# Normed rows transposed inside the last quarter's products, roots on ScalarE alone, and a conv that begins with chunks 0 to 2

## Chip, cores and metric

One core of one Trainium2 chip runs the whole kernel in one launch. The metric is the device time of that core in microseconds (us), the median over the runs shown.

## What is computed

One step of a two-layer encoder over 544 frames of 1024 features: 512 of a new stream and 32 of a running one. Layer 0 is a norm, a combined projection, band attention beside a gated linear recurrence, an output projection and a residual, then a norm and a mixture of experts. Layer 1 has a gated short convolution in place of the mixers. Cut to what the change touches:

```python
def rmsnorm(x, gain):
    y = x * rsqrt(mean(x * x, axis=-1) + 1e-6)
    return y * gain

def short_conv(xn, w_in, conv_w, w_out, prev):      # layer 1
    bg, cg, h = split(xn @ w_in, 3)
    u = cg * h
    up = concat(prev, u)
    conv = up[0:T] * conv_w[0] + up[1:T+1] * conv_w[1] + up[2:T+2] * conv_w[2]
    return (bg * conv) @ w_out

def hier_moe(x, ...):                               # both layers
    grp = argmax(x @ w_group + b_group)             # top 1 of 4 groups
    topv, topi = top_k((x @ w_expert + b_expert)[grp], 2)   # top 2 of its 8 experts
    h = silu(x @ w1[e]) * (x @ w3[e]) * gates       # 32 experts, 1024 -> 256
    return sum over e of h @ w2[e]                  # 256 -> 1024
```

## The kernel before

**Tiling.** Frames lie in five chunks (NC), four of 128 and one of 32 rows (ROWS). H holds the residual stream, one chunk of rows per block. Features are on partitions in eight blocks (KT) for a product, so normed rows are transposed on TensorE first. Float32 products of the mixers are split: a tensor is copied to a rounded high part by ScalarE (..._hi) and the rest is taken by VectorE or GpSimd (..._lo), and three products hi*hi, lo*hi, hi*lo add up in one PSUM bank.

**Norms.** `norm(n, c)` is the norm n (0 and 2 before the mixers, 1 and 3 before the experts) of chunk c. ScalarE's `square` sums squares into ssq (L1036), VectorE makes mean plus epsilon (L1257), ScalarE takes the root (L1038), VectorE the reciprocal (L1259) and the product with row and gain (L1265) into XN (n even) or XF (n odd). For XF the features are re-ordered by the access pattern: it is written densely and H and the gain are read with a step of eight elements. `norm_transpose(n, c)` (L615) then makes eight transposes (L630) into two banks. For n odd ScalarE copies the low and VectorE the high half to XT (L1047, L1270). For n = 2 ScalarE makes xc_hi (L1059) and VectorE xc_lo (L1278).

**Order around the change.** Every engine's order is written out by hand, with semaphores between engines.

- `project_out` (L861): the output projection, in four quarters (OQ) of 256 columns times five chunks, 24 products each (L873), four banks in turn. `residual` on VectorE adds each result to H (L1523); in the last quarter it also calls norm 2n+1 of the chunk before. The splits of the quarters' weights stand in between (L1515).
- `mixture(l)` on TensorE (L883): all five transposes of norm 2l+1, with products of the identity that have no reader (`idle_products`, L613) ahead of chunks 2, 3 and 4; the router's product (L892) over XT; then `route` on VectorE, two small products, and from VectorE's indices GpSimd gathers rows of x from DRAM (L570) for two experts at a time. TensorE transposes these (L927) and runs the 32 experts in pairs (L933, L944).
- The sync queue stores XF's chunks to DRAM (x_rows, L420) as they are normed and loads expert weights into six slots of 24 KB a partition: three transfers of 1 MB an expert (L388 twice, L391). Experts 0 to 3 are sent for ahead of `mixture` (2 and 3 at the start of the last quarter), 4 and 5 behind the router's product, and expert e from 6 on when expert e-6's products are done.
- After the experts of layer 0 the queue reads both results of each row back (yab, L455). VectorE combines them into H (L1682, twice a chunk) with norm 2 of the chunk before in between. TensorE transposes all five chunks, and waits until all are split.
- The conv's products (L1013): a loop of four times two column blocks m, each with two halves of 272 frames; a half has three terms a (banks 3*half + a) of 24 products. ScalarE and VectorE turn each half into gst, g_hi and g_lo; `conv_hi` and `conv_lo` split the weights of coming blocks. `conv_out_hi(0)` and `conv_out_lo(0)` split the first quarter of the next output projection's weights ahead of the conv.

**Memory.** XT lies at 132 KB over XN and the start of XF. The five yab lie at 132 to 172 KB, over XN and XF, where xc_hi (152 KB) also is.

## Time and profile before

| | us |
|---|---|
| median of 3 runs | 1229.3 |
| the three runs | 1226.22, 1229.3, 1235.59 |
| profiled execution | 1231.18 |
| its span on the chip | 1229.4 |
| TensorE products busy | 1035.0 (84%) |
| VectorE busy | 434.6 (35%) |
| ScalarE busy | 282.9 (23%) |
| mean granted clock of TensorE | 0.912 of full |

The views come from one profiled execution. The page sums it up; the chain of waits follows the work that ended last back from the end, at each step to what released it; the timeline gives each instruction with its start, its length, and in brackets how long its engine had been idle and what ended that; windows give busy time, clock and DMA share of a stretch. An engine's busy share over the whole span says little, since the stages have different limits. A product of plain float32 comes as two records (28 for 14 idle products), a transpose as one. A line such as L1265 is a line of the kernel before.

### The profile page before, as it was taken

Reading aid. Unit: us, or ns where it says so; the run is one execution under the profiler, and the core shown is the slowest. Engines: PE = TensorE matmul, PEld = TensorE weight load, DVE = VectorE, ACT = ScalarE, POOL = GpSimd, SP = SyncE. Lnnn points to the kernel's source line nnn. Section 1 sums busy time; section 2 is a strip of 40 time slices with the busy share of each in tenths; the row PEclk is TensorE's granted clock in tenths of the full one; section 3 lists DMA queues with packets and bytes.
Section 4 is the critical chain, followed back from the end, with each engine's and each line's share of the span. In section 5 each row is a group of like instructions: output and inputs, shape, how many; then the busy total and the mean of one; then the engine's idle time right before and its main releaser. Section 6 shows DMA issues by size and latency. Waiting matters only on the chain.

```text
span 1229.4 us, 20254 instructions
## 1 busy us (share of the span) xinstructions
PE 1035.0 (84%) x8691; PEld 807.0 (66%) x8691; DVE 434.6 (35%) x935; ACT 282.9 (23%) x543; POOL 181.2 (15%) x146
## 2 busy tenths in 40 slices
PE   5998999777999899977887179999998899788771
PEld 4988999654599755444443179999997655344440
DVE  5324484357724611101100654655336111010104
ACT  4244322115722121111111322121212121111110
POOL 4234332002000012211111000000000122111110
PEclk9999999856999999989988579999999999988886
DMA  6322321401085769999997703324568699999966
GB/s 213 86 74 69 101 85 38 111 11 52 22 294 194 293 261 416 416 416 416 416 416 286 235 1 103 93 61 154 206 67 353 250 416 416 417 415 417 416 268 227
DMA packets 114855, 282.71 MB, mean 230 GB/s; under 512 B 22954, under 2 KB 70102, under 8 KB 98356
## 3 DMA queue, kind: packets, MB, share of 16 engines
q1 hardware_dynamic: 105044, 263.66, 57.9%
q0 software_dynamic: 9728, 17.85, 3.9%
q8 instruction: 63, 1.03, 0.4%
q14 instruction: 20, 0.16, 0.0%
HBM read 270.57 MB, written 27.02 MB: 242 GB/s over the span
## 4 chain that ended last, share of the span: by engine, by line
PE 57%; DMA 17%; DVE 10%; SPq 10%; ACT 2%; issue 2%; POOL 1%; DVEq 0%; POOLq 0%; ACTq 0%
DMA w<-in_w_dram 13%; PE banks L1013 12%; PE banks L933 11%; PE banks L655 8%; PE banks L873 8%; SPq L388 7%; PE banks L944 4%; PE banks L654 3%; SPq L391 3%; DMA wab<-in_w_in_ab_dram 2%; DVE H L1682 2%; DVE XF L1265 2%; PE banks L927 1%; POOL wab_lo L562 1%; PE banks L832 1%
## 5 line engine op out<-in xcount | busy, mean ns | idle before, releaser
L933 PE MATMUL banks<-w,xgT 128*64 128x256 f32 x2048 | 261.5, 416 | 68.5 <-DMA w<-in_w_dram 67.5
L933 PEld LDWEIGHTS banks<-w,xgT 128*64 128x64 f32 x2048 | 161.3, 150 | 176.9 <-DMA w<-in_w_dram 72.5
L1631 DVE TENSOR_TENSOR hh<-banks,sg 128x128 f32<-128x128 f32 x64 | 18.7, 292 | 410.6 <-ACT sg L1201 377.9
L574 POOL DMA_INDIRECT y_rows<-ys,yidx x64 | 63.8, 996 | 384.7 <-ACT ys L1209 379.8
L944 PE MATMUL banks<-w,hT 128*64 128x512 f32 x512 | 116.9, 598 | 0.0
L1013 PE MATMUL banks<-xc_hi,wc_hi 128*128 128x272 f32 x384 | 111.9, 291 | 1.4 <-DVE xc_lo L1278 1.4
L1013 PE MATMUL banks<-xc_hi,wc_lo 128*128 128x272 f32 x384 | 112.1, 292 | 0.0
L1013 PE MATMUL banks<-xc_lo,wc_hi 128*128 128x272 f32 x384 | 111.6, 291 | 0.0
L570 POOL DMA_INDIRECT xr<-x_rows,gidx x32 | 33.5, 1047 | 430.5 <-DVE yidx L1616 411.9
L655 PE MATMUL banks<-wab_hi,xc_hi 128*128 128x256 f32 (+1 forms) x320 | 91.3, 286 | 0.8 <-POOL wab_lo L562 0.8
L655 PE MATMUL banks<-wab_hi,xp_lo 128*128 128x256 f32 (+1 forms) x320 | 90.3, 283 | 0.0
L655 PE MATMUL banks<-wab_lo,xc_hi 128*128 128x256 f32 (+1 forms) x320 | 88.4, 280 | 0.0
L1201 ACT ACTIVATE sg<-banks 128x128 f32<-128x128 f32 x64 | 17.8, 278 | 296.6 <-PE banks L933 296.6
L562 POOL TENSOR_TENSOR wab_lo<-wab,wab_hi 128x2048 fp32r<-128x2048 f32 x14 | 67.3, 4813 | 122.4 <-ACT wab_hi L1052 122.4
L1013 PEld LDWEIGHTS banks<-xc_hi,wc_hi 128*128 128x128 f32 x384 | 73.5, 191 | 1.6 <-issue 1.5
L1013 PEld LDWEIGHTS banks<-xc_lo,wc_hi 128*128 128x128 f32 x384 | 73.5, 191 | 0.0
L1013 PEld LDWEIGHTS banks<-xc_hi,wc_lo 128*128 128x128 f32 x384 | 73.3, 191 | 0.0
L944 PEld LDWEIGHTS banks<-w,hT 128*64 128x64 f32 x512 | 34.0, 136 | 58.7 <-issue 54.8
L654 PE MATMUL banks<-xc_hi,wab_hi 128*128 128x272 f32 x192 | 57.1, 297 | 7.2 <-POOL wab_lo L562 7.2
L1209 ACT ACTIVATE ys<-banks 128x512 f32<-128x512 f32 x64 | 38.2, 597 | 97.9 <-PE banks L944 97.9
L655 PEld LDWEIGHTS banks<-wab_hi,xc_hi 128*128 128x128 f32 (+1 forms) x320 | 55.7, 174 | 1.7 <-POOL wab_lo L562 1.0
L654 PE MATMUL banks<-xc_hi,wab_lo 128*128 128x272 f32 x192 | 56.8, 296 | 0.0
(284 smaller groups left out, 1811.1 us busy)
## 6 DMA issues: line engine op xcount, KB each, us to landing
w<-in_w_dram SPq DMA_DIRECT2D x192, 1024.0 KB
wab<-in_w_in_ab_dram SPq DMA_DIRECT2D x13, 1024.0 KB, 5.2
wc<-in_w_in_c_dram SPq DMA_DIRECT2D x24, 512.0 KB
yab<-y_rows SPq DMA_DIRECT2D x16, 512.0 KB, 6.9
wo<-in_w_out_ab_dram SPq DMA_DIRECT2D x4, 1024.0 KB, 5.1
x_rows<-XF SPq DMA_DIRECT2D x8, 512.0 KB, 10.4
wo<-in_w_out_c_dram SPq DMA_DIRECT2D x4, 1024.0 KB, 5.7
H<-in_x_prompt_dram SPq DMA_DIRECT2D x4, 512.0 KB, 8.4
```

The lines of the kernel that those rows point to most:

```text
L388: sp.dma_start(w13[s][:, part, :, :], w[l, bass.ds(e, 1)].rearrange("e (p k) f -> p (e k) f", p=P)).then_inc(done, 16)
L391: sp.dma_start(w2s[s][:], w2[l, bass.ds(e, 1)].rearrange("e (a p) n -> p (e a) n", p=P)).then_inc(done, 16)
L562: pool.tensor_tensor(wab_lo[n % 3][:], wab[n % 3][:], wab_hi[n % 3][:].bitcast(F32), ALU.subtract).then_inc(w_lo, 1)
L570: pool.indirect_dma_start(xr[i][:, :], None, x_dram[l][:, :], bass.IndirectOffsetOnAxis(ap=index.bitcast(U32), axis=0), bounds_check=T - 1 ...
L574: pool.indirect_dma_start(y_dram[l][:, :], bass.IndirectOffsetOnAxis(ap=index.bitcast(U32), axis=0), ys[i][:, :], None, bounds_check=4 * T ...
L654: return pe.matmul(out, w[:, k, cols], x[:, k, t], **flags)
L655: return pe.matmul(out, x[:, k, t], w[:, k, :], **flags)
L873: last = pe.matmul(bank[i % 4][0:ROWS[c], 0:OW], z(a, k)[:, c * P:c * P + ROWS[c]], w(b, k, s), start=k == 0 and j == 0, stop=k == KT - 1 ...
L933: last = pe.matmul(bank[hb][64 * f:64 * f + 64, 0:2 * P].rearrange("p (w j) -> p w j", w=2), xgT[i][:, k, 64 * ab:64 * ab + 64], w13[s][:, ...
L944: last = pe.matmul(bank[6 + ab][64 * n:64 * n + 64, :], hT[ab][:, 64 * f:64 * f + 64], w2s[s][:, f, n * 512:(n + 1) * 512], start=f == 0, ...
L1013: last = pe.matmul(bank[3 * half + a][:, 0:HALF], w[s][:, k, a, :], x[:, k, half * HALF:(half + 1) * HALF], start=k == 0 and j == 0, stop= ...
L1209: act.activation(ys[e % 4][:], bank[6 + ab][:, :], ACT.Copy).then_inc(ys_ok, 1)
```

## The change

- **Roots.** ScalarE takes the root straight from ssq, with 1/D as scale and epsilon as bias. VectorE's mean and the semaphore ms_ok go.
- **The view of norms 1 and 3.** H and the gain are read densely and XF is written with a step of 128 elements; its layout is as before.
- **Transposes in the last quarter.** `project_out` calls `norm_transpose` of chunk c-2 behind the products of chunks 2, 3 and 4; chunks 3 and 4 follow in `mixture`. Six idle products stand ahead of chunk 4 and none elsewhere. ScalarE makes all XT copies but the high half of chunk 4.
- **XT** moves into the slot of expert 3, one tensor a layer. Expert 3 is sent for with 4 and 5, behind the router's product.
- **The conv's start.** Combines, norms and splits of chunks 0 to 2 come first, then those of 3 and 4. TensorE begins the first half's terms 0 and 1 when chunks 0 to 2 are split, transposes 3 and 4, runs term 2, and waits for all chunks ahead of the second half. Chunk 2's transposes go to banks 0 and 1. The loop over column blocks is written out. Three of the yab move behind 169 KB.
- **Weights of the output projection in layer 1.** The first quarter's split goes from ahead of the conv to its end.

```diff
--- before.py
+++ after.py
...
+CONV_BANKS = [6, 4, 0, 6, 4]
...
-        XT = at("XT", 132, [P, KT, T])
+        XT = [at(f"XT{l}", RING + 24 * SLOTS[l][3], [P, KT, T]) for l in range(2)]
...
-        yab = [at(f"yab{c}", 132 + 8 * c, [P, 2, D]) for c in range(NC)]
+        yab = [at(f"yab{c}", (132, 140, MISC, MISC + 8, MISC + 16)[c], [P, 2, D]) for c in range(NC)]
...
-                for j in (4, 5):
+                for j in (3, 4, 5):
                     first_load(l, j)
...
-            for j in (2, 3):
-                first_load(0, j)
+            first_load(0, 2)
             mixture(0)
...
-            for j in (2, 3):
-                first_load(1, j)
+            first_load(1, 2)
             mixture(1)
...
             def norm_transpose(n, c):
+                if n % 2 == 1 and c == 4:
+                    idle_products(1, 6)
                 pe.wait_ge(xn_ok, NC * n + c + 1)
-                if n % 2 == 1 and c >= 2:
-                    idle_products(1, 14 if c == 2 else 3)
                 if n == 0 and c == 0:
                     pe.wait_ge(pool_c, zeroed[0])
 
                 low = 6 if c % 2 == 0 else 4
-                if n % 2 == 0 and c > 1:
+                if n == 2:
+                    low = CONV_BANKS[c]
+                if n == 0 and c > 1:
                     pe.wait_ge(xt_d, NC * n + c - 1)
+                if n == 2 and c > 2:
+                    pe.wait_ge(xt_d, NC * n + c - 2)
                 for half in range(2):
                     if n % 2 == 1 and c > 1:
                         pe.wait_ge(xt_a if half == 0 else xt_d, NC * n + c - 1)
...
                     last.then_inc(op_mm, 1)
+                    if s == OQ - 1 and c >= 2:
+                        norm_transpose(2 * n + 1, c - 2)
...
             def mixture(l):
-                norm_transposes(2 * l + 1)
+                for c in (3, 4):
+                    norm_transpose(2 * l + 1, c)
                 pe.wait_ge(xt_a, NC * (2 * l + 2))
...
-                        last = pe.matmul(bank[0][p0:p0 + NR, 0:t.stop - t.start], wr[:, k, :], XT[:, k, t], start=k == 0, stop=k == KT - 1)
+                        last = pe.matmul(bank[0][p0:p0 + NR, 0:t.stop - t.start], wr[:, k, :], XT[l][:, k, t], start=k == 0, stop=k == KT - 1)
...
 
-            norm_transposes(2)
-            pe.wait_ge(xt_a, NC * 3)
-            pe.wait_ge(xt_d, NC * 3)
-            with pe.Fori(0, KT // 2) as i:
-                for s in range(2):
-                    pe.wait_ge(wc_lo_ok, i * 2 + (s + 1))
-                    for half in range(2):
-                        pe.wait_ge(cg_ok, i * 4 + (2 * s + half + 1))
-                        for a in range(3):
-                            for k in range(KT):
-                                for j, (w, x) in enumerate(((wc_hi, xc_hi), (wc_hi, xc_lo), (wc_lo, xc_hi))):
-                                    last = pe.matmul(bank[3 * half + a][:, 0:HALF], w[s][:, k, a, :],
-                                                     x[:, k, half * HALF:(half + 1) * HALF],
-                                                     start=k == 0 and j == 0, stop=k == KT - 1 and j == 2)
-                        last.then_inc(c_mm, 1)
+            def conv_terms(s, half, a):
+                for k in range(KT):
+                    for j, (w, x) in enumerate(((wc_hi, xc_hi), (wc_hi, xc_lo), (wc_lo, xc_hi))):
+                        last = pe.matmul(bank[3 * half + a][:, 0:HALF], w[s][:, k, a, :], x[:, k, half * HALF:(half + 1) * HALF],
+                                         start=k == 0 and j == 0, stop=k == KT - 1 and j == 2)
+                if a == 2:
+                    last.then_inc(c_mm, 1)
+
+            def frames_ready(c):
+                pe.wait_ge(xt_a, NC * 2 + c)
+                pe.wait_ge(xt_d, NC * 2 + c)
+            for c in range(3):
+                norm_transpose(2, c)
+            pe.wait_ge(wc_lo_ok, 1)
+            frames_ready(3)
+            for a in range(3):
+                if a == 2:
+                    norm_transpose(2, 3)
+                    norm_transpose(2, 4)
+                conv_terms(0, 0, a)
+            frames_ready(NC)
+            for a in range(3):
+                conv_terms(0, 1, a)
+            for m in range(1, KT):
+                pe.wait_ge(wc_lo_ok, m + 1)
+                for half in range(2):
+                    pe.wait_ge(cg_ok, 2 * m + half + 1)
+                    for a in range(3):
+                        conv_terms(m % 2, half, a)
...
                 act.activation(junk[:], H[:, c, :], ACT.Square, accum_out=ssq[:, c:c + 1]).then_inc(sq_done, 1)
-                act.wait_ge(ms_ok, NC * n + c + 1)
-                act.activation(rms[:, c:c + 1], rms[:, c:c + 1], ACT.Sqrt).then_inc(rt_ok, 1)
+                act.wait_ge(sq_done, NC * n + c + 1)
+                act.activation(rms[:, c:c + 1], ssq[:, c:c + 1], ACT.Sqrt, bias=epsc[:, 0:1], scale=1.0 / D).then_inc(rt_ok, 1)
...
-            def xt_low(n):
-                for c in range(NC):
-                    act.wait_ge(xt_mm, NXT * n + 2 * c + 1)
-                    act.activation(XT[:, 0:4, c * P:c * P + ROWS[c]],
-                                   bank[6 - 2 * (c % 2)][:, :].rearrange("p (k t) -> p k t", k=4)[:, :, 0:ROWS[c]], ACT.Copy).then_inc(xt_a, 1)
+            def xt_copy(n, c, half, done):
+                act.wait_ge(xt_mm, NXT * n + 2 * c + half + 1)
+                act.activation(XT[n // 2][:, 4 * half:4 * half + 4, c * P:c * P + ROWS[c]],
+                               bank[6 - 2 * (c % 2) + half][:, :].rearrange("p (k t) -> p k t", k=4)[:, :, 0:ROWS[c]], ACT.Copy).then_inc(done, 1)
...
-                    low = 6 - 2 * (c % 2)
+                    low = 6 - 2 * (c % 2) if n == 0 else CONV_BANKS[c]
...
-                squares(2 * l + 1)
-                xt_low(2 * l + 1)
+                for c in range(NC):
+                    square(2 * l + 1, c)
+                    if c >= 2:
+                        xt_copy(2 * l + 1, c - 2, 0, xt_a)
+                        xt_copy(2 * l + 1, c - 2, 1, xt_d)
+                xt_copy(2 * l + 1, 3, 0, xt_a)
+                xt_copy(2 * l + 1, 3, 1, xt_d)
+                xt_copy(2 * l + 1, 4, 0, xt_a)
                 act.wait_ge(lg_mm, 2 * l + 1)
...
-            squares(2)
-            mixer_in_hi(2)
-            conv_out_hi(0)
+            for c in range(3):
+                square(2, c)
+            mixer_in_hi(2, range(3))
+            for c in (3, 4):
+                square(2, c)
+            mixer_in_hi(2, (3, 4))
             for m in range(KT):
                 for half in range(2):
...
                 if m + 2 < KT:
                     conv_hi(m + 2)
+                if m == KT - 2:
+                    conv_out_hi(0)
             mixture(1)
...
             def by_rows(ap):
-                return ap.rearrange("p (q k) -> p k q", k=KT)
+                return ap.rearrange("p (q k) -> p q k", k=KT)
 
             def norm(n, c):
                 gain = gmix if n % 2 == 0 else gffn
-                dve.wait_ge(sq_done, NC * n + c + 1)
-                dve.tensor_scalar(rms[:, c:c + 1], ssq[:, c:c + 1], 1.0 / D, EPS, ALU.mult, ALU.add).then_inc(ms_ok, 1)
                 dve.wait_ge(rt_ok, NC * n + c + 1)
                 tie(dve.reciprocal(rstd[:, c:c + 1], rms[:, c:c + 1]))
                 if c == 0:
                     dve.wait_ge(gmix_in if n % 2 == 0 else gffn_in, 16 * (n // 2 + 1 + 2 * (n % 2)))
                 x, h, g = (XN, XF)[n % 2][:, c, :], H[:, c, :], gain[:]
                 if n % 2 == 1:
-                    x, h, g = x.rearrange("p (k q) -> p k q", k=KT), by_rows(h), by_rows(g)
+                    x, h, g = x.rearrange("p (k q) -> p q k", k=KT), by_rows(h), by_rows(g)
                 dve.scalar_tensor_tensor(x, h, rstd[:, c:c + 1], g, ALU.mult, ALU.mult).then_inc(xn_ok, 1)
...
-            def xt_high(n):
-                for c in range(NC):
...
+            def xt_high(n, c):
+                dve.wait_ge(xt_mm, NXT * n + 2 * c + 2)
+                dve.tensor_copy(XT[n // 2][:, 4:8, c * P:c * P + ROWS[c]],
+                                bank[7 - 2 * (c % 2)][:, :].rearrange("p (k t) -> p k t", k=4)[:, :, 0:ROWS[c]]).then_inc(xt_d, 1)
...
-                    low, t = 6 - 2 * (c % 2), slice(c * P, c * P + ROWS[c])
+                    low, t = 6 - 2 * (c % 2) if n == 0 else CONV_BANKS[c], slice(c * P, c * P + ROWS[c])
...
                 norm(2 * n + 1, NC - 1)
+                xt_high(2 * n + 1, NC - 1)
...
             def mixture(l):
-                xt_high(2 * l + 1)
                 route(l)
...
                 if l == 0:
                     conv_lo(0)
-                for c in range(NC):
-                    n = ROWS[c]
-                    dve.wait_ge(rows_in[c], 16 + 32 * (l + 1))
-                    h = H[0:n, c, :]
-                    for i in range(2):
-                        tie(dve.scalar_tensor_tensor(h, yab[c][0:n, i, :], gate[i][0:n, c:c + 1], h, ALU.mult, ALU.add))
-                    dve.nop().then_inc(h_ok, 1)
-                    if l == 0 and c > 0:
-                        norm(2, c - 1)
-                if l == 0:
-                    norm(2, NC - 1)
+                    for chunks in (range(3), range(3, NC)):
+                        for c in chunks:
+                            combine(l, c)
+                            if c > chunks[0]:
+                                norm(2, c - 1)
+                        norm(2, chunks[-1])
+                        mixer_in_lo(2, xc_lo, chunks)
+                else:
+                    for c in range(NC):
+                        combine(l, c)
+
+            def combine(l, c):
+                n = ROWS[c]
+                dve.wait_ge(rows_in[c], 16 + 32 * (l + 1))
+                h = H[0:n, c, :]
+                for i in range(2):
+                    tie(dve.scalar_tensor_tensor(h, yab[c][0:n, i, :], gate[i][0:n, c:c + 1], h, ALU.mult, ALU.add))
+                dve.nop().then_inc(h_ok, 1)
...
-            mixer_in_lo(2, xc_lo)
             dve.wait_ge(st_in, 48)
             tie(dve.memset(u[:, 0:2], 0.0))
             S0 = 2 + SEQ
             parts = [[(0, HALF, 0)], [(0, SEQ - HALF, HALF), (SEQ - HALF, HALF, SEQ)]]
-            conv_out_lo(0)
...
                     dve.nop().then_inc(cg_ok, 1)
-                    if half == 0 and m + 1 < KT:
-                        conv_lo(m + 1)
+                    if half == 0:
+                        conv_lo(m + 1) if m + 1 < KT else conv_out_lo(0)
```

## Rows read from the trace of the kernel before

**Rows 1.** The page: GB/s in 40 slices of 30.7 us; the instruction queue (packets, MB).

```profile
GB/s 213 86 74 69 101 85 38 111 11 52 22 294 194 293 261 416 416 416 416 416 416 286 235 1 103 93 61 154 206 67 353 250 416 416 417 415 417 416 268 227
...
q8 instruction: 63, 1.03, 0.4%
```

**Rows 2.** Chain of waits, layer 0 and the conv: start us, us, what.

```profile
402.38 2.07 DVE XF L1265
...
409.02 4.09 PE banks L892 x31
...
427.26 5.27 DMA xr<-x_rows,gidx
...
434.57 8.35 PE banks L933 x64
...
447.79 6.91 PE banks L933 x64
...
718.07 147.62 PE banks L1013 x1152
```

**Rows 3.** Timeline, route of layer 0: start us, us, engine, line, what [idle before].

```profile
388.48 0.42 DVE L1523 TENSOR_TENSOR H<-banks,H 128x256 f32<-128x256 f32 x1 [2.43 <-PE banks L873]
...
389.24 0.20 ACT L1038 ACTIVATE rms<-rms 128x1 f32<-128x1 f32 x1 [0.65 <-DVE rms L1257]
...
396.74 1.91 PE L630 MATMUL banks<-ident,XF 128*128 128x128 f32 x16
...
398.73 3.39 PE L613 MATMUL banks<-ident 128*128 128x128 f32 x28
```

**Rows 4.** Timeline between the layers, VectorE and TensorE.

```profile
686.54 2.60 DVE L1682 SCALAR_TENSOR_TENSOR H<-yab,gate,H 128x1024 f32<-128x1024 f32 x2 [5.33 <-DMA yab<-y_rows]
...
690.10 2.60 DVE L1682 SCALAR_TENSOR_TENSOR H<-yab,gate,H 128x1024 f32<-128x1024 f32 x2 [0.96 <-DMA yab<-y_rows]
...
694.82 1.97 PE L630 MATMUL banks<-ident,XN 128*128 128x128 f32 x8 [20.74 <-DVE XN L1265]
...
718.07 0.59 PE L1013 MATMUL banks<-xc_hi,wc_hi 128*128 128x272 f32 x1 [1.38 <-DVE xc_lo L1278]
...
723.67 0.36 PE L1013 MATMUL banks<-xc_hi,wc_hi 128*128 128x272 f32 x1
```

**Rows 5.** Chain of waits, layer 1.

```profile
936.76 4.09 PE banks L892 x31
...
954.92 5.86 DMA xr<-x_rows,gidx
...
962.81 8.76 PE banks L933 x64
```

**Rows 6.** Tiles XF, XN, XT: duration ns min/median/max, first and last start.

```profile
L1265 DVE SCALAR_TENSOR_TENSOR XF<-H,rstd,gffn x10: 2073/2142/2340, 389.7 to 928.5; 128x1024 f32<-128x1024 f32 x10
...
L1265 DVE SCALAR_TENSOR_TENSOR XN<-H,rstd,gmix x10: 1283/1285/3974, 6.7 to 709.0; 128x1024 f32<-128x1024 f32 x10
...
L1047 ACT ACTIVATE XT<-banks x10: 277/591/598, 402.1 to 936.1; 128x512 f32<-128x512 f32 x8, 128x128 f32<-128x128 f32 x2
```

**Rows 7.** Timeline, route of layer 1, TensorE: the first transposes.

```profile
922.12 1.91 PE L630 MATMUL banks<-ident,XF 128*128 128x128 f32 x16
```

**Rows 8.** Windows: us, busy by engine, then PEclk, DMA share, GB/s.

```profile
432.00:436.00 4.00, 2.99 (x18) 1.91 (x20) 0.69 (x1) 1.88 (x2) 0.99 (x1) 0.71 0.05 18
...
933.00:937.00 4.00, 3.57 (x25) 3.30 (x25) 1.18 (x3) 0.88 (x2) 0.00 (x0) 0.70 1.02 418
```

**Rows 9.** Tile xr, all 32 gathers; DMA queues in 452 to 454 us (packets, MB, share).

```profile
DMA to landing us min/median/max: 3.4/8.4/10.0
...
q0 software_dynamic: 65, 0.17, 21.3%
```

**Rows 10.** Timeline of the sync queue: the seventh expert's first transfer.

```profile
439.50 0.80 SPq L388 DMA_DIRECT2D w<-in_w_dram  x2
```

**Rows 11.** Timeline: TensorE's longest pause with no cause shown.

```profile
243.70 0.43 PE L749 MATMUL banks<-st,qdecT 64*32 64x64 f32 x7 [4.35 <-issue]
```

More of the change, by code:

```diff
@@ L241, in hmoe_step @@
         h_ok = sem("h_ok")
-        sq_done = sem("sq_done"); ms_ok = sem("ms_ok"); rt_ok = sem("rt_ok")
+        sq_done = sem("sq_done"); rt_ok = sem("rt_ok")
         xn_ok = sem("xn_ok"); xt_mm = sem("xt_mm"); xt_a = sem("xt_a"); xt_d = sem("xt_d")
@@ L1263, in norm @@
                 if n % 2 == 1:
-                    x, h, g = x.rearrange("p (k q) -> p k q", k=KT), by_rows(h), by_rows(g)
+                    x, h, g = x.rearrange("p (k q) -> p q k", k=KT), by_rows(h), by_rows(g)
                 dve.scalar_tensor_tensor(x, h, rstd[:, c:c + 1], g, ALU.mult, ALU.mult).then_inc(xn_ok, 1)
-            def xt_high(n):
-                for c in range(NC):
-                    dve.wait_ge(xt_mm, NXT * n + 2 * c + 2)
-                    dve.tensor_copy(XT[:, 4:8, c * P:c * P + ROWS[c]],
-                                    bank[7 - 2 * (c % 2)][:, :].rearrange("p (k t) -> p k t", k=4)[:, :, 0:ROWS[c]]).then_inc(xt_d, 1)
+            def xt_high(n, c):
+                dve.wait_ge(xt_mm, NXT * n + 2 * c + 2)
+                dve.tensor_copy(XT[n // 2][:, 4:8, c * P:c * P + ROWS[c]],
+                                bank[7 - 2 * (c % 2)][:, :].rearrange("p (k t) -> p k t", k=4)[:, :, 0:ROWS[c]]).then_inc(xt_d, 1)
             def mixer_in_lo(n, lo, chunks=range(NC)):
                 for c in chunks:
-                    low, t = 6 - 2 * (c % 2), slice(c * P, c * P + ROWS[c])
+                    low, t = 6 - 2 * (c % 2) if n == 0 else CONV_BANKS[c], slice(c * P, c * P + ROWS[c])
                     dve.wait_ge(xt_a, NC * n + c + 1)
```

## The prediction

> **What bounds the kernel now.** I read the page first, then the chain of waits in order of time, then the timeline, the windows and the tiles of the three places that the diff touches. The page shows that the weight stream is at 416 GB/s for most of both expert stages [rows 1]; the chain shows TensorE elsewhere, with three gaps in which it waits for a norm [rows 2 to 5]. An expert stage that starts earlier moves all behind it, because each expert transfer from the seventh on is released by a product: a gap closed by x us is worth x us, unless the stream takes it back.
>
> Gap 1, route of layer 0. The projection's last product ends at 396.7, where transposes start [rows 3]; the router starts at 409.02 [rows 2]. In between VectorE is the chain: five norms, one per 3.2 us, each an add, a mean, a root on ScalarE, a reciprocal and a pass of 2.1 to 2.3 us; the last pass ends at 404.45, and two XT copies, idle products and the transposes of chunks 3 and 4 follow one another for 4.6 us [rows 2, 3, 6].
>
> Gap 2, ahead of the conv. Five pairs of combines (2.60 a pair), five norms, serial transposes and splits; the first conv product is at 718.07, and until 723.67 the products run at 1.2 GHz [rows 4].
>
> Gap 3, route of layer 1, is gap 1 again but longer: from 922.12 to the router at 936.76 [rows 5, 7], the clock partly down [rows 8].
>
> **The change, gap 1.** The root comes from ssq by scale and bias, so the mean on VectorE and its hand-overs go. Today the add ends at 388.90, the root runs at 389.24 to 389.44 after a wait for the mean of 0.65, and by the chain's pattern the pass starts 0.24 later, at 389.68 [rows 3]. Reciprocal straight behind the add puts it at 389.3: 0.4 us less a norm. ScalarE is ahead, as that wait shows. The norm's view changes from reads of every eighth element and a dense write to dense reads and a write to every 128th. No row shows such a write. It is bounded by the dense norm, 1.28, and today's form, 2.14 [rows 6]; I take the middle of what the two ends give. The Trainium skill ("SBUF — State Buffer", Specifications) states 16-byte lines in SBUF that want two hits each for full bandwidth; today's reads agree (2.14 against 1.28), and by that rule the new write misses each time and the pass keeps its 2.1 us.
>
> The schedule. Transposes of chunks 0, 1, 2 (0.96 each, half of 1.91) stand behind the last quarter's third, fourth and fifth product; products are 2.43 + 0.42 = 2.85 apart [rows 3]. Third product to 391.1, T0 to 392.1, fourth to 395.0, T1 to 396.0, fifth to 398.7, T2 to 399.7; the add of chunk 4 ends at 399.4. Fast pass: norm 3 to 401.0, T3 to 402.1, norm 4, whose root is there at 401.2, to 402.7, six idle products (12 of 28 records that take 3.39: 1.45) to 403.5, T4 to 403.9, copy 0.28 [rows 6], hand-overs of 0.3 and 0.4: router at 404.7. Slow pass: norm 3 to 402.1, T3 to 403.1, norm 4 to 404.4, router at 405.9. The gain is 4.3 or 3.1; I take 3.6. The other XT copies fall in ScalarE's waits between squares.
>
> **What the route gives back.** XT now lies in an expert slot, so expert 3's 3 MB leave the last quarter, where they cost nothing, and go out with 4 and 5 when the router's products end. Before, that is 6 MB at 413.1, some 15 us at 416 GB/s, and the first gather, issued at 427.26, meets only the tail: TensorE has its rows 5.3 us later, and in layer 1 5.9 [rows 2, 5]. With 9 MB the engines are full for 22.7 us from about 409.7, past 432, and the gather goes out at 423.6, in the thick of it. Gathers take 3.4 to 10.0 to landing, 8.4 in the median, because beside a full stream their queue gets 21% of the engines' time [rows 9]. I take 8.5: 3.2 us lost in layer 0, 2.6 in layer 1; bounds 0 and 4.7 (10.0 - 5.3). The transfer itself is covered: the queue has nothing more until the first product frees a slot, at 439.5 [rows 10], and expert 3 is wanted only after three experts' products.
>
> A second, smaller price: TensorE stands while it waits for the rows; the clock is at 0.71 in 432 to 436 [rows 8], and the first pair's products take 8.35 (layer 1: 8.76) where later ones take 6.91 [rows 2, 5]. A wait 3 us longer lets the clock fall for good. What a cold start costs the conv shows: 25 products in 5.6 us, 0.224 each [rows 4], against (147.62 - 5.60) / 1127 = 0.126 [rows 2], so 2.5 us. That is 1.1 more than now in layer 0 and 0.6 in layer 1; bounds 0 and 2.5.
>
> Layer 0 in sum: 3.6 - 3.2 - 1.1 = -0.7.
>
> **Gap 2.** VectorE now does combines, norms and splits of chunks 0 to 2, then the rest. With 0.4 less a norm, from [rows 4]: combine 1 ends at 692.7, norm 0 at 694.3, combine 2 at 696.9 (its rows are there if chunks keep coming 3.6 apart, as at 686.54 and 690.10), norm 1 at 698.5, norm 2 at 700.0. T2, 1.97 at 1.2 GHz, ends at 702.5, ScalarE's halves at 703.4, the split at 704.8: first conv product at 705.2, 12.9 us earlier. Two terms, still cold at first, run to 713.8. Meanwhile VectorE does combines 3 and 4 to 710.0 and the norms to 713.3, so T3 and T4 find their rows and cost TensorE 1.4; term 3 runs to 718.2 while chunks 3 and 4 are copied and split to about 718.0. Net 12.9 - 1.4 = 11.4 with rounding. The reserve at the second half is 0.2 us, so a late norm goes straight into the sum; bounds 8 and 12.5. The first out-projection weights' two splits move to the end of the conv, behind conv products of 9 us a half of which these engines need about a third; uncovered they would delay the projection by their own length. The loop written out adds no work.
>
> **Gap 3.** The same schedule from a last product at 922.1 + 1.9 for T0 and T1: router at 930.1 or 931.0 instead of 936.76, since the waits for banks and the cold transposes go too. I take 6.2 between 6.7 and 5.8. Net 6.2 - 2.6 - 0.6 = 3.0. One expert less ahead of the x stores is worth nothing: the gather waits for the indices.
>
> The first norms too are 0.4 shorter each, but what follows them waits for weights: nothing.
>
> **Sum.** -0.7 + 11.4 + 3.0 = 13.7 us. The profiled execution took 1231.18 (span 1229.4), so 1217.5. It stands 1.9 above the median of 1229.3, and from that the forecast is 1215.6.
>
> **Rivals.**
> A. The gather is not slowed (27%). For: it already goes out under load in both layers, and no scatter is ahead of it. Against: its queue's 21% beside full weights [rows 9]. Then 3.6 + 11.4 + 6.2 = 21.2: 1208.1. The Trainium skill ("DMA: Bandwidth & Descriptors", Queues, rings and completion order) says that an engine takes turns between its queues packet by packet; an even turn would bring the gather's 0.5 MB in 2.5 us and give this time. The 21% disagrees.
> B. The conv starts early but stumbles (13%): chunk 2's rows come late, or the second half waits for chunks 3 and 4. With half of 11.4 lost, 1221.3.
> C. The clock falls in the route (13%). TensorE stands 1.5 to 2.2 us ahead of T3 and has 6 idle products where there were 20; in layer 1 it is at 0.70 there even now [rows 8]. T3, idle products, T4 and router at half speed cost 2.8 + 4.1 = 6.9 a layer: 1229.4.
> D. Slower: the written-out conv starves TensorE of instructions (5%). It has 864 more pairs in the program; 1.03 MB were fetched for 20254 instructions [rows 1], so these are some 88 KB, six fetches of 16 KB. TensorE once stands 4.35 us for nothing that the profile shows [rows 11]. Six of these give 26: 1241.7; from 2.3 us a fetch it is slower than before. Against: the projection's written-out products stand 2.85 apart without a gap [rows 3].
>
> Main case 42%, its own range 1211 to 1220.
>
> **How the numbers follow.** One per cent is 12.3 us: faster is below 1217.0, slower above 1241.6, about what a measurement here can tell from no change. Faster: A, and some three fifths of the main case, with a little of B: 0.55. Same: the rest of these and C, 0.40. Slower: D, 0.05. The range goes from 1204, A with the upper bound of the conv and the fast pass, to 1227, most of C; it leaves out D, part of C and a tail of A.
>
> **What would show it.** Right: 18.7 us from the first combine to the first conv product, and no wait before the second half; first gathers at 8 to 9 us to landing; first pair's products at 9 us or more. A pass of XF near 1.3 or 2.1 settles the view. Wrong: a gather at 5 (A), a conv wait on xc_lo in its first block (B), a clock under 1.00 around the router (C), idle "issue" in the conv (D).

## Result, and the profile after

| | before | changed |
|---|---|---|
| median, us | 1227.91 (8 runs) | 1218.97 (8 runs, 1216.57 to 1224.76) |
| ratio, 95% interval | | 0.9929, 0.9903 to 0.9955 |
| profiled execution, us | 1231.18 | 1220.05 |
| its span, us | 1229.4 | 1218.3 |

The change makes the kernel 0.7% faster, 0.45% to 0.97% by the interval: clear of no change, but under 1%, which the prediction called the same. A second set of six runs of it (experiment e8) gave 1217.3 and a ratio of 0.9908, 0.9886 to 0.9929.

The chain of waits of the changed kernel, in order of time (start, length in us, what): route of layer 0, the conv, route of layer 1.

```profile
388.02 2.09 DVE XF L1293
404.06 4.09 PE banks L898 x31
422.33 9.71 DMA xr<-x_rows,gidx
432.08 1.97 PE banks L933 x8
434.95 8.46 PE banks L939 x64
...
704.60 9.04 PE banks L1011 x48
713.64 1.48 PE banks L633 x16
715.12 138.91 PE banks L1011 x1104
...
899.83 4.59 another core or an unknown queue
...
918.78 2.27 PE banks L612 x12
922.47 5.72 PE banks L898 x31
942.27 9.09 DMA xr<-x_rows,gidx
...
954.26 8.22 PE banks L939 x64
```

Against [rows 2, 3, 5]: from the first pass over XF to the router, layer 0 takes 404.06 - 388.02 = 16.04 us where it took 409.02 - 389.68 = 19.34. Then more than the gain is handed back: the gather is 9.71 us long instead of 5.27, the transposes of its rows 1.97 instead of 1.09, and from the first pass to the first expert product it is 46.93 us where it was 44.89. The conv's first product is at 704.60, 13.5 earlier, and the rest of the conv runs without a wait behind the last transposes (1104 products in 138.91). In layer 1 the chain has two lines that were not there: 4.59 ahead of VectorE's second add with no cause shown (the adds beside it wait 2.43 for their products, so 2.2 are a pause), and a router of 5.72 instead of 4.09.

The conv's start in the timeline (start, length, engine, line, operation, and in brackets the idle time before and what ended it):

```profile
687.64 5.36 DVE L1720 SCALAR_TENSOR_TENSOR H<-yab,gate,H 128x1024 f32<-128x1024 f32 x4 [4.92 <-DMA yab<-y_rows]
704.60 0.56 PE L1011 MATMUL banks<-xc_hi,wc_hi 128*128 128x272 f32 x1 [2.10 <-DVE xc_lo L1305]
```

First combine to first conv product is 16.96 us, against 718.07 - 686.54 = 31.53 before [rows 4]. From here to the projection of layer 1 the second column block and those behind it run as before, so this gap's gain stays.

The windows of the route (us, busy time and instructions of PE, PEld, DVE, ACT and POOL, then granted clock, DMA share and GB/s), changed kernel:

```profile
424.00:428.00 4.00, 1.69 (x16) 1.50 (x14) 0.00 (x0) 0.00 (x0) 0.84 (x1) 1.00 1.03 423
428.00:432.00 4.00, 0.00 (x0) 0.00 (x0) 0.00 (x0) 0.00 (x0) 0.00 (x0) 0.86 1.01 409
432.00:436.00 4.00, 3.53 (x16) 2.41 (x18) 0.69 (x1) 1.88 (x2) 0.99 (x1) 0.50 0.57 221
436.00:440.00 4.00, 4.00 (x33) 2.67 (x31) 0.00 (x0) 0.00 (x1) 0.00 (x0) 0.79 0.29 71
```

While TensorE has nothing at all to do, from 428 to 432, the DMA engines carry 409 GB/s. By queue (packets, MB, share of the engines' time), q1 has the weights and q0 the gather; the changed kernel in 428 to 430 and in 430 to 432:

```profile
q1 hardware_dynamic: 89, 0.69, 82.9%
q0 software_dynamic: 84, 0.16, 21.9%
...
q1 hardware_dynamic: 106, 0.50, 61.5%
q0 software_dynamic: 108, 0.28, 35.9%
```

The gather does move beside the weights, about packet for packet, but its packets are small: 0.16 MB in 84 of them against 0.69 MB in 89. The weights go on until about 434.3, two microseconds after the first rows are there. TensorE starts at 0.50 of its clock, the 1.2 GHz level, where it stood at 0.71 in this window before [rows 8].

### The profile page after: what moved, and what is told of

It is laid out like the page before. It is cut to its first block, busy times and chain, and to the rows that moved or that the text cites. A ratio compares the mean times of both kernels' runs of the same rounds, so it can differ in the third digit from the quotient of the medians.

```text
span 1218.3 us, 20101 instructions
## 1 busy us (share of the span) xinstructions
PE 1028.2 (84%) x8635; PEld 799.6 (66%) x8635; DVE 426.3 (35%) x907; ACT 289.6 (24%) x551; POOL 181.0 (15%) x146
## 3 DMA queue, kind: packets, MB, share of 16 engines
q8 instruction: 70, 1.15, 0.4%
## 4 chain that ended last, share of the span: by engine, by line
PE 59%; DMA 15%; SPq 12%; DVE 7%; ACT 2%; issue 2%; POOL 1%; another core or an unknown queue 0%; DVEq 0%; POOLq 0%; ACTq 0%
PE banks L1011 12%; PE banks L939 11%; DMA w<-in_w_dram 10%; PE banks L876 9%; PE banks L658 8%; SPq L389 8%; PE banks L950 5%; SPq L392 3%; PE banks L657 3%; DMA wab<-in_w_in_ab_dram 2%; DMA xr<-x_rows,gidx 2%; PE banks L933 1%; PE banks L633 1%; DMA yab<-y_rows 1%; POOL wab_lo L561 1%
## 5 line engine op out<-in xcount | busy, mean ns | idle before, releaser
L1658 DVE TENSOR_TENSOR hh<-banks,sg 128x128 f32<-128x128 f32 x64 | 18.7, 292 | 407.2 <-ACT sg L1226 407.2
L658 PEld LDWEIGHTS banks<-wab_hi,xp_lo 128*128 128x128 f32 (+1 forms) x320 | 55.8, 174 | 0.4
```

The source lines that it names most:

```text
L658: return pe.matmul(out, x[:, k, t], w[:, k, :], **flags)
```

## Experiments

**Theories.** T1: the gather is slow because three experts' weights (9 MB) go out ahead of it, and this eats what the early transposes gain. Its rival: the gather's length has another cause, and the transposes are worth what the prediction said. T2: TensorE's clock, down after the longer waits, costs microseconds of its own. Its rival: expert stages are set by the weight stream, so a faster first pair is worth nothing.

### One expert behind the gather (e1)

```diff
-                for j in (3, 4, 5):
-                    first_load(l, j)
+                for j in (3, 4):
+                    first_load(l, j)
+                sp.wait_ge(xr_in[0], 16 * (PAIRS // 2 * l + 1))
+                first_load(l, 5)
```

> The changed kernel, but expert 5's three transfers wait for the first gather's rows; 3 and 4 go out behind the router's product as before. Stream theory (the gather is slow because 9 MB of weights are in flight): with 6 MB in flight, as in the kernel before, the rows are at TensorE 5.3 to 5.9 us after the gather's issue instead of 9.7 and 9.1, their transposes take 1.1 instead of 1.97, and expert 5 fills the hole that the stream has at 430 to 440; first expert product some 4 to 5 us earlier in each layer, so 6 to 9 us faster than the changed kernel (1219.0): 1210 to 1213. Rival (the gather is slow for another reason, such as the x rows stored just ahead of it): 9 us again, and 1219 to 1222.

Measured: 1209.85 us, ratio 0.9854 (0.9823 to 0.9885). Its chain and two windows:

```profile
389.76 2.10 DVE XF L1295
405.82 4.09 PE banks L900 x31
424.07 5.23 DMA xr<-x_rows,gidx
431.34 7.13 PE banks L941 x64
...
914.05 4.09 PE banks L900 x31
932.21 5.31 DMA xr<-x_rows,gidx
939.56 7.13 PE banks L941 x64
```

```profile
424.00:428.00 4.00, 3.43 (x31) 3.24 (x29) 0.87 (x5) 0.00 (x0) 2.21 (x2) 1.00 0.95 361
428.00:432.00 4.00, 2.06 (x16) 1.52 (x18) 0.69 (x1) 1.88 (x2) 0.79 (x1) 1.00 0.60 178
```

The gather is back at 5.23 and 5.31, the clock stays at 1.00, and the first pair takes 7.13. First pass to first expert product: 41.58 us instead of 46.93. The rival falls: the length of the gather goes with the weights that are ahead of it. The clock is less sure a gain: e7 below has the same wait ahead of the rows, 1.9 us, and there it fell.

### All three behind the gather (e2)

The same edit with 3, 4 and 5 all behind the wait.

> The changed kernel with the transfers of experts 3, 4 and 5 all behind the first gather's rows. Stream theory: nothing is in flight, the gather takes 3.4 to 4.5 us, but the stream stands from about 409 to 427 instead of from 432 to 439.5, and the expert stage ends when its stream ends: 8 to 10 us later a layer less the 5 that its start gains, so 5 to 12 us slower than the changed kernel, 1224 to 1231. Rival, the expert stage is set by its products and not by the stream: 8 to 10 us faster, 1209 to 1211.

Measured: 1240.83 us, ratio 1.0101 (1.007 to 1.0131). The gather alone took 4.37, as expected; against the changed kernel the loss was 21.9 us, about twice my upper estimate of 12. Windows of this run (columns as above):

```profile
420.00:424.00 4.00, 3.34 (x34) 3.18 (x35) 3.13 (x15) 0.00 (x0) 0.77 (x1) 1.00 0.00 0
...
428.00:432.00 4.00, 3.41 (x31) 2.53 (x31) 0.69 (x1) 1.88 (x2) 0.99 (x1) 1.00 0.74 268
```

No weights move from 409 to 428, and the stage from first expert product to first combine is 429.63 to 698.36 = 268.7 us, where it is 252.7 in the changed kernel and 251.8 in e1: 16 us for a later start of the stream. So the stream does set the expert stage, and one expert's transfers behind the gather are free only because the stream has a hole there anyway.

### More idle products (e3)

```diff
-                if n % 2 == 1 and c == 4:
-                    idle_products(1, 6)
+                if n % 2 == 1 and c >= 3:
+                    idle_products(1, 10)
...
-                idle_products(4, 22)
+                idle_products(4, 46)
```

> The changed kernel with idle products that fill TensorE's waits: ten ahead of the transposes of chunk 3 and of chunk 4 (6 ahead of 4 alone before), 46 instead of 22 ahead of the first gather's rows. Clock theory: granted clock 1.00 through the router of layer 1 (4.1 us instead of 5.72) and through the transposes of the first gathered rows (1.1 instead of 1.97) and the first pair's products (6.9 instead of 8.46 and 8.22); 2.5 us in layer 0 and 4 in layer 1, less 0.5 a layer by which the added products outlast a wait: about 5 to 6 us faster, 1213 to 1214. Rival, the head start is lost again because the stream sets the end of each expert stage: the rows show the faster pieces but the time is within 2 us of 1219.

Measured: 1213.83 us, ratio 0.9879 (0.9856 to 0.9902). The gather stays slow, the clock does not fall:

```profile
423.70 9.15 DMA xr<-x_rows,gidx
434.89 7.13 PE banks L939 x64
...
917.30 4.09 PE banks L898 x31
935.46 9.91 DMA xr<-x_rows,gidx
947.41 7.13 PE banks L939 x64
```

The clock theory's number, 1213 to 1214, is what came: 5.1 us below the changed kernel, 3.5 below its second measurement (e8, whose interval overlaps). The faster first pair is not handed back in full: from the end of the pair to the first combine layer 0 takes 243.8 us, where the changed kernel took 244.2 and 243.0 in its two profiles. That it counts because it frees the slots from which the stream goes on is argued, not shown.

### The changed kernel without its early transposes (e4)

In `project_out` the call of `norm_transpose` goes, `mixture` has all five again, XT lies at 132 KB, and experts 3 and 4, 5 are sent as before the change.

> The changed kernel with the transposes of norms 1 and 3 put back behind the last quarter, XT back at 132 KB, the high XT copies back on VectorE, expert 3 sent in the last quarter and idle products as before; roots on ScalarE, the norm's view and the conv's early start stay. What the trace says: the early transposes gained 3.7 us ahead of the router and lost 4.4 to 5.3 at the gather in layer 0, and gained 1.0 and lost 4.1 in layer 1. So without them the kernel should be 2 to 4 us faster than the changed kernel, 1215 to 1217 (the conv's 12.8 stay). Rival, the theory of the prediction (early transposes are worth 2.3 us net): 1221 to 1222.

Measured: 1212.12 us, ratio 0.9873 (0.9845 to 0.9902), against 0.9929 and 0.9908 with them: the early transposes, as they were built, cost 4 to 7 us (e8's interval just overlaps e4's). They are the one part of the change that loses. The timeline says why so little stood on their other side: with the root on ScalarE alone the passes over XF keep pace with the products. e4's chain, route of layer 0:

```profile
388.96 2.10 DVE XF L1287
391.81 2.10 DVE XF L1287
...
399.52 2.03 DVE XF L1287
406.03 4.09 PE banks L897 x31
424.29 5.07 DMA xr<-x_rows,gidx
```

The five passes are 2.85 apart (2.74 and 2.12 at the end), the pace of a product, where they were 3.4 apart before [rows 2]. First pass to router is 17.07, against 19.34 before and 16.04 with the early transposes: of 3.3 us the roots and the view brought 2.3, the transposes 1.0. The gather of layer 1 took 7.02 us in this run and 6.72 in e5, against 5.86 before. Both send experts 2 and 3 in the last quarter, as the kernel before, but reach the router sooner, and then the sync queue still waits for the stores of XF's rows (here what it waited for between 915 and 925: us in total, times, longest):

```profile
SPq L389 <- DMA x_rows<-XF: 1.5, 1, 1.5
```

So experts 4 and 5 go out 1.6 us behind the router's end (1.1 in e5, 0.1 before and in e1), and the gather meets more of them. With one expert less ahead of the stores, e1's gather took 5.31.

### Roots and view alone (e5), conv alone (e6)

Each is put into the kernel before by itself.

> The kernel before with the roots straight from ssq on ScalarE and the norm's new view, and nothing else. From the two traces: with it the passes of the norms ahead of the router start 2.85 apart, the pace of the projection's products, instead of 3.4, so VectorE keeps up with TensorE; from the first such pass to the router 17.1 us instead of 19.3 in layer 0 and 16.7 instead of 20.9 in layer 1, and five norms ahead of the conv at 0.4 each. That is 2.3 + 4.2 + 2.0 = 8.5, of which the gather may take back 1 to 2: 1220 to 1222 against 1228.2. The prediction priced it at some 2 us a gap (five norms at 0.4), so 1222. Rival, the norms are hidden behind the products and only the tails count: 1 us a gap, 1225.

> The kernel before with the conv's early start alone (order of combines, norms and splits, banks, the written-out loop, yab, the output weights' split at the end); roots, view, transposes and expert loads as before. The trace of the changed kernel says 12.8 us for the gap, of which 2 are the five shorter norms, so 10.8 here: 1217 to 1218. With e5 it should add up to the 16 us of the changed kernel without the early transposes. Rival: the earlier start is partly given back in layer 1, 1221 or more.

Measured: e5 1220.8 us, ratio 0.9939 (0.9916 to 0.9962); e6 1219.26 us, ratio 0.992 (0.9895 to 0.9945). By the ratios that is 7.5 and 9.8 us, together 17.3, and e4, which has both, is 15.6 us below its kernel before (by the medians 7.1, 8.7 and 16.1). Within the intervals the parts add up. In e6 the conv's first product comes 17.93 us after the first combine, but chunks 3 and 4 are late, since each norm is 0.4 longer:

```profile
710.57 0.36 PE L1010 MATMUL banks<-xc_hi,wc_hi 128*128 128x272 f32 x1 [2.10 <-DVE xc_lo L1301]
717.78 1.09 PE L635 MATMUL banks<-ident,XN 128*128 128x128 f32 x8 [0.90 <-DVE XN L1289]
719.60 0.68 PE L635 MATMUL banks<-ident,XN 32*128 32x32 f32 x8 [0.72 <-DVE XN L1289]
```

So 31.53 - 17.93 = 13.6, less 1.6 of waits and 1.8 of transposes inside the conv: 10.2 from the schedule. From the first combine to the projection e6 in fact gained 12.6 (692.64 to 859.19 against 686.54 to 865.70); the other 2.4 are the clock, granted at 1.00 in the conv's first 4 us where it was at 0.50 before and in the changed kernel (0.62 in e8, 0.65 in e1; what decides it was not found). e5, with the shorter norms alone, gained 2.7 in this gap, and with the 10.2 that makes the 12.8 of the changed kernel to 0.1. The two waits are not there in it: the shorter norms pay for the conv's reserve.

### Dense norms (e7), and the changed kernel again (e8)

```diff
-                if n % 2 == 1:
-                    x, h, g = x.rearrange("p (k q) -> p q k", k=KT), by_rows(h), by_rows(g)
...
-                            last = pe.transpose(bank[half][:, kk * P:(kk + 1) * P], xr[i][:, k * P:(k + 1) * P], ident[:])
+                            last = pe.transpose(bank[half][:, kk * P:(kk + 1) * P], xr[i][:, :].rearrange("p (q k) -> p k q", k=KT)[:, k, :], ident[:])
```

e7 is e1 with this, and the same step in the transposes of XF.

> The kernel with one expert behind the gather, and norms 1 and 3 dense on both sides: XF keeps its features in order, and TensorE's transposes of XF and of the gathered rows take every eighth column instead. If a dense pass takes 1.28 as the conv's norms do, the two passes behind the last product save 0.8 each and the others fall in the products' shadow: 1.6 us a layer, 3 in all, 1206 to 1207 against 1209.9. Rival, TensorE's weight load pays for the step of 32 bytes: 256 transposes of gathered rows and 80 of XF get longer; at twice the time they cost 0.13 us each, on the chain in the parts of the expert stages where TensorE is behind: slower than 1209.9.

> The changed kernel itself, with a second profile. In the first, VectorE's second add of the last quarter stood 2.2 us for nothing that the profile shows, TensorE's clock fell ahead of the router of layer 1 (router 5.72 us), and layer 1's route gained 1.0 us where layer 0's gained 3.7. If the early transposes themselves bring that, it is there again, with the gather at 9 to 10 us in both layers. If it is chance, the router takes 4.09 in layer 1 and only the gathers of 9 to 10 us are there again. Time 1217 to 1220 either way.

Measured: e7 1206.47 us, ratio 0.9823 (0.9791 to 0.9854). The tile view of XF, first e1, then e7 (duration in ns: least, median, most):

```profile
L635 PEld LDWEIGHTS banks<-ident,XF x80: 136/140/144, 391.9 to 913.4; 128*128 128x128 f32 x64, 32*128 32x128 f32 x16
...
L1295 DVE SCALAR_TENSOR_TENSOR XF<-H,rstd,gffn x10: 1990/2067/2115, 389.8 to 910.6; 128x1024 f32<-128x1024 f32 x10
```

```profile
L636 PEld LDWEIGHTS banks<-ident,XF x80: 180/193/208, 393.0 to 916.0; 128*128 128x128 f32 x64, 32*128 32x128 f32 x16
L636 PE MATMUL banks<-ident,XF x80: 269/274/376, 393.1 to 916.1; 128*128 128x128 f32 x64, 32*128 32x32 f32 x16
L1294 DVE SCALAR_TENSOR_TENSOR XF<-H,rstd,gffn x10: 1283/1285/1286, 391.3 to 913.0; 128x1024 f32<-128x1024 f32 x10
```

The pass falls from 2.07 to 1.28, and the weight load with a step rises from 140 to 193 ns, hidden behind the product's 274. The route gains less than I expected: from the add of chunk 1 to the router 16.28 us instead of 16.83 in layer 0 (0.55, where one pass saves 0.8 and I had counted two), and the clock was down for the first pair (8.81 us instead of 7.13). The profiled spans are equal at 1206.7, and the two intervals overlap; e7's median is 3.4 us lower, but that e7 beats e1 is not shown.

e8: 1217.3 us. VectorE's pause was chance: its engine had stood 4.67 us ahead of this add, and stands 2.4 to 3.8 there in the other eleven profiles, each time for the product. The clock's fall ahead of layer 1's router came again, with a router of 5.63 and a gather of 8.88, and layer 0's gather took 9.66:

```profile
421.89 9.66 DMA xr<-x_rows,gidx
...
918.77 5.63 PE banks L898 x31
938.48 8.88 DMA xr<-x_rows,gidx
```

### The two put together (e9, e10)

> The dense kernel (e7) with the transposes of norms 1 and 3 back behind the last quarter, XT at 132 KB, expert 3 sent in the last quarter, 4 behind the router's product and 5 behind the first gather's rows. It asks what the early transposes are worth once their bill at the gather is gone. By the traces the early transposes put the router 1.0 us earlier in layer 0 and 0.6 in layer 1; here only 3 MB are in flight at the gather, so its rows should be there in 4.4 to 5 us instead of 5.3: about even with e7, 1206 to 1208. Rival, TensorE's 40 transposes in a row are on the chain once the norms are shorter: 4 us a layer less the 1.6 that the norms' tail saves: 1210 or more.

> The dense kernel (e7) with ten idle products ahead of the transposes of chunk 3 and of chunk 4 instead of six ahead of 4, and 30 instead of 22 ahead of the gather's rows. In e7 the first pair's products took 8.81 and 8.00 us where later ones take 6.91; with the wait for the rows (1.91 us) filled they should take 7.1: 1.3 a layer, less 0.5 by which the products ahead of chunk 4 outlast its norm: 1.5 to 2 us faster than e7, 1204 to 1205. Rival: TensorE is ahead of the stream in the expert stage, so a faster first pair brings nothing and only the outlasting counts: 1207.

Measured: e9 1209.07 us, ratio 0.9837 (0.9806 to 0.9868); e10 1208.52 us, ratio 0.9834 (0.9811 to 0.9857). With the bill at the gather gone, the early transposes are the 1.7 us between e9 and e7 by the ratios (2.6 by the medians), inside the intervals and so not shown to be worth anything. In e9 the gather, with one expert ahead of it, took 4.10 in layer 0. In e10 the first pairs took 7.13 instead of 8.81 and 8.00, but two groups of idle products of 2.23 us stood on the chain ahead of the router; the two cancel. e1, e7, e9 and e10 can't be told apart; all are some 1.5 to 1.8% below the kernel before, and 0.5 to 1% below the changed kernel.

## Why the prediction came out right, and where its steps did not

**The total.** Predicted 13.7 us off, 1215.6; measured 8.9 by the medians, 11.1 by the two profiled executions. The time lies in the range, and in the main case's own, but these are wide (23 and 9 us), the gain by the medians is two thirds of the forecast, and the outcome that was held likelier, more than 1% off (0.55), did not come. That the sum is no further out owes something to luck: gap 2 gave more than its term, while gaps 1 and 3 gave less. The parts (gap 1 to the router is counted from the first pass, 3.3, or from the add of chunk 1, 3.7; gap 2 from the first combine to the projection):

| step | predicted | measured |
|---|---|---|
| gap 1, to the router | +3.6 | +3.3 to +3.7 |
| gap 1, gather | -3.2 | -4.4 |
| gap 1, cold start | -1.1 | -1.0 (0.9 at the transposes, 0.1 at the pair) |
| gap 2, conv | +11.4 | +12.8 (e6 alone: 12.6, of which 2.4 are the clock) |
| gap 3, to the router's end | +6.2 | +1.0; +2.8 in e8 |
| gap 3, gather and cold start | -3.2 | -3.2 and -0.3; -3.0 and -0.4 in e8 |

**Gap 1: the way to the router right in size, its source not.** The prediction gave the roots 0.4 a norm and saw the gain in the transposes that no longer stand in a row. e4 and e5 show 2.3 of the 3.3 us in layer 0 from roots and view, since VectorE had been slower than the products (3.4 against 2.85 a chunk) and now is not. No run takes root and view apart; the five passes alone are 10.4 us in e4 against 11.0 before, so most of it is the root's shorter way. The gather's term was under-sized by 1.2: I took 8.5 us, about the median landing, and the rows came after 9.75 (432.08 - 422.33). Its first packet moved 4.4 to 4.7 us after the issue, where it was 1.8 to 2.0 with nothing in flight (e2) and 2.2 to 2.7 behind 6 MB (e1, before), for a reason that no run shows; and from 427 to 432 it had 14 to 45% of the engines' time in each microsecond. In e1 the weights are through at 427, the gather then has 60 to 77%, and the rows come at 429.3; in e2 they take 4.37. The cold start had its size, but not where I put it: the first pair took 8.46 us, not 9 or more, and 0.9 of the 1.0 fell on the transposes.

**The pass over XF.** I took the middle of 1.28 and 2.14; it is 1.99 to 2.11 us in the changed kernel. The step moved from the reads to the write and costs the same. The rule cited ahead (the Trainium skill, "SBUF — State Buffer", Specifications: two hits in a 16-byte line) agrees, for reads and for writes, and with 1.285 when neither side has a step.

**Gap 2.** The place and the mechanism were right: 16.96 us from first combine to first product where 18.7 was forecast, no wait before the second half, 1.48 for the two transposes. Of the 1.7 us, 0.8 lie in the combines (chunk 1's results were back, so four run as one group of 5.36, where I had 6.16 to the end of the second pair; in e8 they came later, and the gap was 17.90) and 0.6 in the splits (2.10 after the last transpose, not 2.7).

**Gap 3 is the step that failed.** From the start of the projection to the router the kernel before took 71.06 us, e5 66.39, e4 66.30, e1 65.68. So roots and view alone, which e5 has and which I had priced at 0.4 a norm, give 4.7 of the 5.4 here; the early schedule, from which I drew the 6.2, adds 0.6. In the changed kernel it is 68.44: against e1 the chance pause puts TensorE 1.5 us later at the first transposes, from chunk 3's transposes to the router it takes 1.3 more at the lower clock, and the router itself takes 5.72. That is rival C, the clock falling in the route, which had 13% and came true in layer 1 alone. Windows of e8 and of e1, the second shifted by 3.33 us so that both hold the same work:

```profile
910.00:914.00 4.00, 2.04 (x19) 1.76 (x17) 2.98 (x6) 2.78 (x6) 0.00 (x0) 1.00 0.74 301
914.00:918.00 4.00, 4.00 (x27) 3.77 (x28) 1.95 (x1) 1.19 (x4) 0.00 (x0) 0.64 0.47 164
```

```profile
906.67:910.67 4.00, 2.03 (x19) 1.76 (x17) 2.97 (x6) 2.79 (x6) 0.00 (x0) 1.00 0.80 327
910.67:914.67 4.00, 3.57 (x34) 3.26 (x36) 2.44 (x3) 1.42 (x4) 0.00 (x0) 1.00 0.47 165
```

In e8 TensorE stands 1.96 us ahead of chunk 3's transposes, and in the window behind it has 0.64 of its clock, for six idle products and the last transposes (and 0.51 in the window with the router). e1 has the same work up to here, stands 1.97 us at the same place, and stays at 1.00. In e2 the clock fell at this place too, but was back for the router (4.09). What decides between them was not found. In the two profiles with ten idle products ahead of chunks 3 and 4 (e3, e10) the clock stayed up, at 1 us on the chain. One sentence of the prediction fell besides: that one expert less ahead of the x stores is worth nothing. In e4 and e5 the stores did hold up the loads behind them, by 1.6 and 1.1 us.

**Rivals A and D.** A (gather not slowed) fell: 9.7 and 9.1 us. The rule named beside it (the Trainium skill, "DMA: Bandwidth & Descriptors", Queues, rings and completion order), an engine's turn between its queues packet by packet, agrees with the trace by the packet: 84 packets against 89, then 108 against 106. What fell is my reading of it as an even turn of bytes: the gather's 84 packets carried 0.16 MB, the weights' 89 carried 0.69. D (a written-out conv starving TensorE) fell too: the page has 70 instruction packets of 1.15 MB instead of 63 of 1.03, and 1104 products run in 138.91 us, 0.126 each, as before.

**The size of what can be seen.** The add of chunk 1 in layer 0's last quarter stands between 386.83 and 392.18 us in the twelve profiles, ahead of nearly all that these kernels change; the clock at the conv's start is worth up to another 2.4. Some microseconds of one profile's total are thus not the change's, and gaps must be measured from their own start, as in the table. Its right column adds up to 8.6 of the 11.1 us between the two profiled executions; of the other 2.5, 1.2 stand ahead of gap 1 and the rest is in the two expert stages behind their first pairs (0.6 lost in layer 0, 2.0 gained in layer 1, cause not found).

## What to carry to other kernels

A buffer that moves into a prefetch slot moves a transfer too: ask which small, urgent transfer is then behind it, and send only as much ahead of that one as will have nearly drained when it goes out. Let the rest wait for it, if the stream has a hole there anyway; if it has none, most of the time that the stream stands comes back at the end of the stage (16 us for some 19 in e2). And before building around a slow engine, take the small thing off its chain: one op and one hand-over less a chunk, with the new view, brought 7.5 us in a few lines, where the rearranged transposes brought 1.0 and 0.6 and lost 4.4 and 3.2 at the gathers behind them.

## What was not expected of the hardware

- A gather of 0.5 MB took 4.37 us with the DMA engines idle, 5.1 to 5.9 behind two experts' weights that were nearly through, and 8.9 to 9.9 behind three. Its queue moved about as many packets as the weights' queue (84 against 89 in 428 to 430), but of 1.9 KB instead of 7.8, and so had 22% of the engines' time there.
- A weight load of TensorE that reads float32 at every eighth column takes 193 ns instead of 140 and is hidden behind a product of 274.
- TensorE's clock was at its lower level in one layer's route and not in the other's, and in one kernel and not in another, with the same instructions ahead of it: 5.63 and 5.72 us against 4.09 for the same router.
